# Query and key projections by seven block products, behind the value projections

## The reference, cut to what matters

```
h = rms_norm(x, pre_norm_gain)
proj = h @ w_in                        # (256, 1024) @ (1024, 9344 columns in all)
q, k, v = proj[..., :4608]             # three groups of 8 heads of 64 each: 1536 columns q, 1536 k, 1536 v
#   dilated attention in three groups (stride 1, 4, 16), logits = q k^T / 8 + bias,
#   joined over the groups by one softmax; o_attn * silu(z_attn) @ w_up_attn
r, k, v, w_low, a_low = shifted(proj[..., OFF_RWKV:OFF_RWKV_GATE])
#   RWKV-7 recurrence over the tokens, group norm, bonus; o_rwkv * silu(z_rwkv) @ w_up_rwkv
merged = sigmoid(g_attn) * y_attn + sigmoid(g_rwkv) * y_rwkv
x = x + rms_norm(merged @ w_out, post_norm_gain)
# second block: a projection, a Hyena mixer (filters, transforms, gates), differential attention,
# w_out_2, router, and 16 experts of 1024 x 2816 (gate, up, down), 32 tokens each: some 550 MB of weights
```

## Time and profile before

| | |
|---|---|
| median of 3 runs | 1835.41 us (1835.23 to 1835.87) |
| profiled execution | 1837.94 us, its span 1835.8 us |
| mean granted clock of TensorE | 0.855 of full |
| PE busy | 1375.2 us, 75% |
| PE weight loads busy | 769.3 us, 42% |
| DVE busy | 435.8 us, 24% |
| ACT busy | 144.8 us, 8% |
| POOL busy | 36.4 us, 2% |
| chain that ended last | PE 53%, DMA 33% |
| L890 (project) | 976 instructions of 256 columns, 221.6 us |

### The profile page before, as it was taken

One profiled execution on the slowest core, in us unless ns is written; L12 is line 12 of the kernel. 1 busy time (PEld: TensorE's weight loads), 2 busy tenths in 40 slices (PEclk: granted clock), 3 DMA queues, 4 the chain that ended last, 5 costly groups with the idle time before them and its releaser, 6 DMA issues.

```text
span 1835.8 us, 21606 instructions
## 1 busy us (share of the span) xinstructions
PE 1375.2 (75%) x10034; PEld 769.3 (42%) x10034; DVE 435.8 (24%) x671; ACT 144.8 (8%) x316; POOL 36.4 (2%) x53
## 2 busy tenths in 40 slices
PE   9999999999999865756666674756656575766655
PEld 7888577858665321313222231322322131322311
DVE  3543224357653211010102101010210101021012
ACT  3200012113131000000000000000000000000001
POOL 1001010000000000000000000000000000000000
PEclk9999999999999978777787787878787787778788
DMA  7324363333389999999999999999999999999995
GB/s 256 138 94 144 110 224 117 112 127 111 124 328 392 430 435 429 432 432 428 436 430 431 432 431 430 427 434 432 427 434 432 430 433 426 430 434 431 431 428 238
DMA packets 54909, 629.55 MB, mean 343 GB/s; under 512 B 3546, under 2 KB 4741, under 8 KB 37412
## 3 DMA queue, kind: packets, MB, share of 16 engines
q1 hardware_dynamic: 51952, 620.02, 80.4%
q0 software_dynamic: 2448, 7.82, 1.5%
q10 hardware_dynamic: 420, 0.34, 0.1%
HBM read 627.05 MB, written 1.11 MB: 342 GB/s over the span
## 4 chain that ended last, share of the span: by engine, by line
PE 53%; DMA 33%; another core or an unknown queue 8%; DVE 4%; ACT 1%; issue 1%; POOL 0%; POOLq 0%; DVEq 0%; SPq 0%; ACTq 0%
DMA arena<-in_w_up 25%; PE psum L1453 12%; PE psum L890 12%; PE psum L1503 6%; DMA arena<-in_w_gate 5%; PE psum L1442 4%; PE psum L1232 3%; DMA arena<-in_w_down 3%; PE psum L1162 2%; PE psum L1321 2%; PE psum L893 2%; PE psum L969 1%; DVE arena L2109 1%; PE psum L896 1%; PE psum L1136 1%
## 5 line engine op out<-in xcount | busy, mean ns | idle before, releaser
L1453 PE MATMUL psum<-arena 128*32 128x352 f32 x4096 | 418.8, 573 | 335.3 <-DMA arena<-in_w_up 207.3
L1453 PEld LDWEIGHTS psum<-arena 128*32 128x32 f32 x4096 | 149.7, 133 | 604.4 <-issue 246.2
L1503 PE MATMUL psum<-arena 128*32 128x512 f32 x1408 | 230.7, 729 | 48.0 <-DMA arena<-in_w_down 48.0
L890 PE MATMUL psum<-arena 128*128 128x256 f32 x976 | 221.6, 383 | 1.3 <-ACT arena L601 0.7
L890 PEld LDWEIGHTS psum<-arena 128*128 128x128 f32 x976 | 181.9, 189 | 29.8 <-issue 2.2
L2102 DVE TENSOR_SCALAR arena<-arena 128x704 f32<-128x704 f32 x16 | 8.4, 528 | 639.6 <-ACT arena L836 639.5
L1503 PEld LDWEIGHTS psum<-arena 128*32 128x32 f32 x1408 | 67.1, 128 | 198.2 <-issue 122.9
L2109 DVE TENSOR_TENSOR arena<-psum,arena 128x704 f32<-128x704 f32 x16 | 21.5, 1345 | 318.2 <-PE psum L1453 318.2
L1442 PEld LDWEIGHTS psum<-arena 128*128 128x128 f32 x512 | 93.1, 285 | 1.5 <-issue 1.1
L1442 PE MATMUL psum<-arena 128*128 128x32 f32 x512 | 93.4, 357 | 0.2 <-DVE arena L2066 0.2
L839 ACT ACTIVATE arena<-psum 128x1024 f32<-128x1024 f32 x15 | 15.4, 1024 | 775.1 <-PE psum L1503 775.1
(11 more groups left out here) (373 smaller groups left out, 970.0 us busy)
## 6 DMA issues: line engine op xcount, KB each, us to landing
arena<-in_w_gate SPq DMA_DIRECT2D x22, 5632.0 KB, 53.8
arena<-in_w_up SPq DMA_DIRECT2D x21, 5632.0 KB, 52.1
arena<-in_w_down SPq DMA_DIRECT2D x19, 5632.0 KB, 54.6
arena<-in_w_up SPq DMA_DIRECT2D x21, 2816.0 KB, 48.1
arena<-in_w_down SPq DMA_DIRECT2D x20, 2816.0 KB, 54.1
arena<-in_w_gate SPq DMA_DIRECT2D x20, 2816.0 KB, 50.2
arena<-in_w_in SPq DMA_DIRECT2D x24, 2048.0 KB, 8.7
arena<-in_w_down SPq DMA_DIRECT2D x11, 1408.0 KB, 50.4
```

Source lines behind the costliest of these rows:

```text
L890: last = mm(o, block_of(blk)[:, k, c * P:c * P + P], rhs[:, k, :], start=(k == 0), stop=(k == KC - 1))
L1453: last = mm(psum[32 * j:32 * j + CAP, b + n, 0:HALFQ], XC[:, k, :], region(o, HALFQ), start=(k == 0), stop=(k == KC - 1))
L1503: last = mm(psum[32 * g:32 * g + CAP, gate + 1 - n, :], HT[:, i, :], region(spot(pos), 512), start=(i < 4), stop=(i >= FPP - 4))
```

## The change

For the six blocks q0 to q2 and k0 to k2 the product (512 columns by 1024 features) x (1024 features by 256 tokens) is cut into 2 x 2 blocks (256 columns, 512 features, 128 tokens) and done with seven block products and sums, one level of Strassen's scheme in Winograd's form, in place of eight. Tiles 19 to 42 are now q and k, each block in four parts: A, B and C hold two block products in one bank, D one. GpSimd makes the sums of the weights (S1, S2, and two in place) and of the tokens (T1 to T4, once for hT, once for hR). ScalarE copies the first product of A, VectorE adds all the others out of PSUM. S1, S2 and T1 to T4 take the place of slot 1, so q and k blocks alternate between slots 2 and 0. The value blocks come before q and k, as tiles 13 to 18. The gates, tiles 43 to 50, come behind the chain and all before the transposes of Y. The factor 0.125 moves into `biased`. GpSimd's bias DMAs stand behind its sums.

In the diff below `summed` is one tensor_tensor on GpSimd and a wait for its own end. After the lists and counts come GpSimd's part, ScalarE's (`evac` returns at once for B, C and D), TensorE's and VectorE's. In the state phase whole tiles 37 to 42 stand where halves of 37 to 40 stood, and `halves_added` stands once behind each step of VectorE.

```
+        S1, S2 = region(4096, 4, 256), region(5120, 4, 256)
+        T1, T2, T3, T4 = (region(6144 + 512 * i, 4, P) for i in range(4))
...
+        blocks += [(f"v{i}", in_cols(w_in, 3072 + 512 * i)) for i in range(3)]
         blocks += [(f"q{i}", in_cols(w_in, 512 * i)) for i in range(3)]
         blocks += [(f"k{i}", in_cols(w_in, 1536 + 512 * i)) for i in range(3)]
-        blocks += [(f"v{i}", in_cols(w_in, 3072 + 512 * i)) for i in range(3)]
...
+        SLOTS = (0, 2, 1, 0, 2, 1, 0, 2, 0, 2, 0, 2, 0)
+        def slot_of(n):
+            return SLOTS[n] if n < len(SLOTS) else (n + 1) % NB
+        def tenant_before(n):
+            if blocks[n][0] == "g0":
+                return "k2"
+            return next((blocks[i][0] for i in reversed(range(n)) if slot_of(i) == slot_of(n)), None)
...
+        tiles += [(f"q{i}", c, hT, qT[:, 4 * i:4 * i + 4, :], 1.0) for i in range(3) for c in "ABCD"]
+        tiles += [(f"k{i}", c, hR, kT[:, 4 * i:4 * i + 4, :], 1.0) for i in range(3) for c in "ABCD"]
+        assert (V_TILE, Q_TILE, Z_TILE, G_TILE, NT) == (13, 19, 43, 51, 67)
+        def seven(j):
+            return Q_TILE <= j < Z_TILE
+        def evacs(j):
+            return sum(not seven(i) or tiles[i][1] == "A" for i in range(j + 1))
+        def halves(j):
+            return sum(seven(i) for i in range(j + 1))
+        def sums_at(j):
+            blk, c = tiles[j][0:2]
+            n = SEVEN.index(blk)
+            if blk == "k0":
+                return 23 if c == "B" else 24
+            return 4 + 4 * n + (4 if n > 3 else 0) + (2 if c == "B" else 4)
...
+            def token_sums(h):
+                summed(T1, h[:, 0:4, P:T], h[:, 0:4, 0:P], ALU.subtract)
+                summed(T2, h[:, 4:KC, P:T], T1, ALU.subtract)
+                summed(T3, h[:, 4:KC, P:T], h[:, 0:4, P:T], ALU.subtract)
+                summed(T4, T2, h[:, 4:KC, 0:P], ALU.subtract)
+            def weight_sums(name):
+                w, j = block_of(name), first_of(name)
+                weights_in(pool, name)
+                if j > Q_TILE:
+                    pool.wait_ge(S["proj_ready"], j - 2)
+                summed(S1, w[:, 0:4, T:2 * T], w[:, 4:KC, T:2 * T], ALU.add)
+                summed(S2, S1, w[:, 0:4, 0:T], ALU.subtract)
+                summed(w[:, 0:4, T:2 * T], w[:, 0:4, 0:T], w[:, 0:4, T:2 * T], ALU.subtract)
+                if name == "k0":
+                    pool.wait_ge(S["proj_ready"], j)
+                    token_sums(hR)
+                pool.wait_ge(S["proj_ready"], j + 1)
+                summed(w[:, 4:KC, 0:T], w[:, 4:KC, 0:T], S2, ALU.subtract)
+            pool.wait_ge(S["proj_ready"], first_of("q0"))
+            token_sums(hT)
+            for name in SEVEN:
+                weight_sums(name)
             pool.wait_ge(S["T1_mm"], 5)
...
+                if seven(j):
+                    act.activation(quarter(j, 0, 1), part(j, 0), ACT.Copy).then_inc(S["proj_evac"], 1)
+                    return
...
             from_state(1)
-            evac(36)
-            evac(37)
             from_state(2)
-            evac(38)
+            evac(39)
             from_state(3)
-            evac(39)
-            evac(40)
-            evac(41)
             act.wait_ge(S["mean_in"], 3)
             act.activation(small[:, 64:80], small[:, 64:80], ACT.Sqrt).then_inc(S["root_in"], 1)
-            for j in range(42, 47):
+            for j in range(Z_TILE, 47):
                 evac(j)
...
+            def block_product(j, slot, w, h):
+                for f in range(2):
+                    o = psum[:, bank_of(j), slot * T + f * P:slot * T + f * P + P]
+                    for k in range(4):
+                        last = mm(o, w[:, k, f * P:f * P + P], h[:, k, :], start=(k == 0), stop=(k == 3))
+                return last
+            def seven_products(j):
+                blk, c, h = tiles[j][0:3]
+                w = block_of(blk)
+                if c in "BC":
+                    pe.wait_ge(S["w_sums"], sums_at(j))
+                if c == "A":
+                    block_product(j, 0, w[:, 0:4, 0:T], h[:, 0:4, 0:P])
+                    last = block_product(j, 1, w[:, 4:KC, 0:T], h[:, 4:KC, 0:P])
+                elif c == "B":
+                    block_product(j, 0, S2, T2)
+                    last = block_product(j, 1, S1, T1)
+                elif c == "C":
+                    block_product(j, 0, w[:, 0:4, T:2 * T], T3)
+                    last = block_product(j, 1, w[:, 4:KC, 0:T], h[:, 4:KC, P:T])
+                else:
+                    last = block_product(j, 0, w[:, 4:KC, T:2 * T], T4)
+                last.then_inc(S["proj_ready"], 1)
...
             project(18)
-            project(19)
...
                 if cp:
+                    project(19)
                     project(20)
                     pe.wait_ge(S["gram_done"], 5)
...
             solve(3)
-            project(40, 0, 4)
+            project(43, 0, 4)
             step(3)
-            project(40, 4, 8)
-            for j in range(41, 47):
+            project(43, 4, 8)
+            for j in range(44, G_TILE):
                 project(j)
             pe.wait_ge(S["gn_done"], 1)
...
-            for j in range(47, G_TILE):
-                project(j)
...
+            def halves_added(j):
+                c = tiles[j][1]
+                left, right = part(j, 0), part(j, 1)
+                c11, c12, c21, c22 = (quarter(j, i, t) for i in range(2) for t in range(2))
+                if c == "A":
+                    dve.wait_ge(S["proj_evac"], evacs(j))
+                    last = V.tensor_tensor(c11, right, c12, ALU.add)
+                else:
+                    dve.wait_ge(S["proj_ready"], j + 1)
+                    dve.wait_ge(S["half_read"], halves(j - 1))
+                if c == "B":
+                    link(V.tensor_tensor(c12, left, c12, ALU.add))
+                    last = V.tensor_tensor(c22, right, c12, ALU.add)
+                elif c == "C":
+                    link(V.tensor_tensor(c21, left, c12, ALU.add))
+                    link(V.tensor_tensor(c12, right, c22, ALU.add))
+                    last = V.tensor_tensor(c22, left, c22, ALU.add)
+                elif c == "D":
+                    last = V.tensor_tensor(c21, c21, left, ALU.subtract)
+                last.then_inc(S["half_read"], 1)
...
+                if cp:
+                    halves_added(19)
+                    halves_added(20)
                 dve.wait_ge(S["gram_mm"], 2 * cp + 1)
...
                     link(V.tensor_tensor(flat(mOff), flat(mA), over(OFFB[lev + 1]), ALU.mult))
+                halves_added(24 + 2 * lev)
                 dve.wait_ge(S["MM_mm"], lev + 1)
...
                     mirrored(2 * lev + 4)
+                halves_added(25 + 2 * lev)
...
-                link(V.tensor_tensor(LG[:, i, :, :], psum[:, 2 * i:2 * i + 2, 0:384], bias[:, tile, 2 * p:2 * p + 2, :], ALU.add))
+                link(V.scalar_tensor_tensor(LG[:, i, :, :], psum[:, 2 * i:2 * i + 2, 0:384], 0.125, bias[:, tile, 2 * p:2 * p + 2, :], ALU.mult, ALU.add))
```

More of the change, by code:

```diff
@@ L397, in program, with weights_in @@
         number = {name: n for n, (name, _) in enumerate(blocks)}
+        SLOTS = (0, 2, 1, 0, 2, 1, 0, 2, 0, 2, 0, 2, 0)
+        assert number["v1"] == 5 and number["k2"] == 12
+        def slot_of(n):
+            return SLOTS[n] if n < len(SLOTS) else (n + 1) % NB
         def block_of(name):
-            return wb[(number[name] + 1) % NB]
-        def weights_in(pe, name):
+            return wb[slot_of(number[name])]
+        def weights_in(eng, name):
             n = number[name]
-            pe.wait_ge(wload[(n + 1) % NB], 16 * (n // NB + 1))
+            eng.wait_ge(wload[slot_of(n)], 16 * sum(slot_of(i) == slot_of(n) for i in range(n + 1)))
+        def tenant_before(n):
+            if blocks[n][0] == "g0":
+                return "k2"
+            return next((blocks[i][0] for i in reversed(range(n)) if slot_of(i) == slot_of(n)), None)
         experts = [A[n].rearrange("e (p i) n -> (e p) (i n)", p=P) for n in ("w_gate", "w_up", "w_down")]
@@ L416, in program @@
         tiles += [(f"rkv{i}", c, hT, prT[:, 4 * i + c, :], 1.0) for i in (1, 0, 2) for c in range(4)]
-        Q_TILE = len(tiles)
-        tiles += [(f"q{i}", c, hT, qT[:, 4 * i + c, :], 0.125) for i in range(3) for c in range(4)]
-        tiles += [(f"k{i}", c, hR, kT[:, 4 * i + c, :], 1.0) for i in range(3) for c in range(4)]
         V_TILE = len(tiles)
@@ L439, in program, with first_of @@
         tiles2 += [(f"at{i}", c) for c in range(4) for i in (0, 1)]
+        SEVEN = ("q0", "q1", "q2", "k0", "k1", "k2")
+        def first_of(name):
+            return min(j for j, t in enumerate(tiles) if t[0] == name)
+        def sums_at(j):
+            blk, c = tiles[j][0:2]
+            n = SEVEN.index(blk)
+            if blk == "k0":
+                return 23 if c == "B" else 24
+            return 4 + 4 * n + (4 if n > 3 else 0) + (2 if c == "B" else 4)
         def bank2_of(j):
```

(31 more changed lines are left out.)

61 lines of the change are left out of this document (41 added, 20 removed).

## The result

The changed kernel takes 1841.14 us (median of 7 runs, 1840.52 to 1841.69) against 1835.23 for the kernel before (7 runs in the same comparison, 1834.74 to 1835.87): a ratio of 1.0032 (95% interval 1.0020 to 1.0043), 5.9 us slower. The prediction said 1837.3 with a range of 1830 to 1843. The time lies in the range, but past the 0.2% that were to count as no change, on the side that had a chance of 0.32. All comparisons use fast runs; two executions of the kernel before beside the last four experiments, at 2100.59 and 2702.36 us, are left out.

What follows compares the result with a forecast made beforehand. TensorE was taken to bound the kernel up to about 555 us, the expert stream after it. -8.1 - 0.1 + 3.9 + 3.4 + 0.2 + 2.6 = +1.9 us on 1835.4 gave 1837.3, range 1830 to 1843.

Steps and rivals of the forecast that it cites:

- Parts 1 and 2: TensorE's q and k products and the value tiles moved ahead: -8.1 and -0.1 us for the products, 0 for the moves.
- Part 3: TensorE waits before product B of q0 for six GpSimd sums of 10.2 us: +3.9 us, bounds 0 and 9.8.
- Part 5: Gates behind the chain: TensorE waits at tile 45 for ScalarE's group norm square root and table load, +3.4 us.
- transposes at tile 52: Transposes of Y right before logits(0), VectorE doing orT and zaT before the first biased: +0.2 us.
- Part 4: VectorE's adds, seven a block at 0.42 us, and ScalarE's evacuations are covered by TensorE's work: 0.
- Part 6: TensorE's clock falls behind each of the two new waits, three in four, 1.7 us a fall: +2.6 us.
- rival (b): TensorE's clock stays down longer, 6.8 us behind each wait, losing 3.4 each: 1841.5 us; chance 0.14.
- Part 1: Seven products a block, 112 instructions at 0.1115 us for 64 at 0.2162: -8.1 us over six blocks, another -0.1 for placing.
- Rival (d): Products don't save what they say: at 0.124 us an instruction of 128 columns no gain, 1845.4 us; chance 0.03.
- (a): GpSimd is fast: its six sums end before B, only the second wait is left, 1830.8 to 1832.5 us; chance 0.18.
- (c): GpSimd is slow, 3.75 ns an element: waits of 9.8 + 1.6 in place of 3.9, 1844.8 us; chance 0.09.
- Rival (e): One of the two waits is hidden by something not seen: 1832.6 or 1832.1 us; chance 0.14.

Runs made afterwards that it cites:

- the last four experiments: Changed kernel, waits filled with matmuls: 1836.9 us; its order with eight products: 1835.3; kernel before with 16 GpSimd adds: 1836.04; with 16 copies: 1836.5.
- the four kernels that have them: The changed kernel, and it with one edit: tile 18 earlier, 1836.01 us; tiles 43 and 44 evacuated earlier, 1836.09; q1's sums held back, 1837.08.
- the kernel with eight products: The changed kernel's tile order with the plain product, no sums or adds, tiles 43 and 44 evacuated before the square root: 1835.3 us.
- the three together: The changed kernel with tile 18 before the bonus matmuls, tiles 43 and 44 evacuated before the square root, q1's sums held back: 1827.84 us.

## Why the prediction was right or wrong

| step | predicted | measured |
|---|---|---|
| Parts 1 and 2, products and moves | -8.2 | -7.5 (products -7.9, moves +0.4) |
| Part 3, first wait | +3.9 | +3.8 |
| Part 5, second wait | +3.4 | +3.15 |
| Part 5, transposes at tile 52 | +0.2 | 0 |
| Part 4, VectorE's additions | 0 | +2.2 |
| Part 6, clock | +2.6 | +4.2 (4.7 by the medians) |
| sum | +1.9 | +5.9 |

That the time lies in the range is partly luck: the range reached that far up for rival (b), a clock that stays down longer, while the miss of 3.8 us is as large as a wait that no rival had, with its fall of the clock (2.2 + 1.6).

**Part 4 failed**, at the words "If such cover were gone, each place would cost what the adds last, 0.4 to 1.4 us. I put 0." It took VectorE's durations from the trace of before, where GpSimd is nearly idle in this stretch, and added up VectorE's own load. The adds did fit, if only just: all of them are in the experiment that holds back q1's sums, and they cost TensorE 0.2 us there, not 2.2. The part names the places where the cover is tightest; tile 23, behind tile 21's three additions, is not among them, and there it was used up. What did not stay was the duration of a VectorE instruction beside a busy GpSimd. The critical one grew from 1.22 to 3.27 us. The state phase itself had no such wait, as predicted; the third wait stands just ahead of the levels, a place for which the prediction had no sign of its own. The Trainium skill, SBUF — State Buffer, section "SBUF: two separate sides", states the rule that the prediction should have weighed: a VectorE instruction with two SBUF inputs and a GpSimd instruction that reads SBUF share a pair of ports under an exclusive lock, and whoever starts second waits until the first is through. The trace agrees: 2.05 us of delay that end with GpSimd's sum, none where an input is in PSUM, and a GpSimd mean of 2.57 us in place of 2.36 where the two are mixed.

**Part 6 was mis-sized**, 2.6 for 4.2. More than a third of it (1.6) is Part 4's again, since the third wait has its own fall of the clock. The price of a wait, 0.75 x 1.7 = 1.3 us, is near what the runs show (1.4 to 1.6), and three waits by it give 3.9. The trace has the fall behind six of the nine idle waits of 2.2 to 3.8 us in the four kernels that have them, the price being 1.6 to 2.6 us when it comes. Which wait it follows is not fixed: the one at tile 45 has none in the changed kernel and one in two experiments. The Trainium skill, TensorE: Matmul & The Clock Gate, part 1, has idling take the clock back, and the prediction read that as a fall behind each wait. These traces don't bear that reading out at this length of wait: three of the nine have none. What settles it for a single wait stays open.

**Part 1.** 2 x 4 matmuls a product and 7 products a block are as counted. An instruction is 0.1117 us from the next, (3.84 - 0.377) / 31, where 0.1115 was taken, and D, 16 instructions, takes 2.05, with 1.98 to the start of what follows (238.31, 240.29). Six blocks of 112 instructions at 0.1117 in place of 64 at 0.2162 make 8.0. The bill has 7.5, and the 0.4 us between them is what the changed order costs by itself in the trace of the kernel with eight products (553.87 against 553.49). Rival (d) is out.

**Part 3** was right in structure and in size: six sums took 9.8 us (108.19 to 118.02; 10.2 predicted), 1024 elements 2.36 (2.33), 512 elements 1.28 and 1.10 by turns (1.36). The chain of waits lays them end to end ahead of the product:

```profile
112.07 1.10 POOL arena L587
...
113.24 2.36 POOL arena L587
115.67 2.35 POOL arena L587
...
118.15 6.40 PE psum L966 x32
```

Its estimate from a one-input and a strided copy was good; rivals (a) and (c) are out. The later blocks' sums are covered as it said, their bias DMAs too (issued from 228.55).

**Part 5** was right: step(3) ends at 246.29, the table load and the first evacuation stand where it put them, and TensorE restarts 8.6 us behind (233.3 - 224.67 = 8.6 predicted). ScalarE's timeline:

```profile
252.57 0.22 ACT L756 ACTIVATE arena<-arena 128x16 f32<-128x16 f32 x1 [13.54 <-DVE arena L1826]
252.81 1.28 ACT L705 ACT_TABLE_LOAD   x1
254.10 0.39 ACT L705 ACTIVATE arena<-psum 128x256 f32<-128x256 f32 x1
```

The 0.2 us at tile 52 did not come: the wait ahead of it is 0.56 us where it was 0.57, and the distance to the kernel before is 5.9 us in front of it and behind it. Rival (e), one of the two waits hidden, is out: both are in the trace, and the second went when ScalarE's order was changed. Rival (b) is the nearest in its number (1841.5), and for half of its reason: the clock did stay down 6.8 us behind the first wait in the profiled execution. It was down 3.4 behind the others, or not at all, so as a rule it did not hold; the number came from a third wait.

**The end of the span.** That a microsecond of TensorE's before 555 us is one of the end is borne out: +5.9 at 559.39 and +5.9 on the medians; for the three together, against the changed kernel, -12.9 in the trace (546.45) and -13.3 on the medians. The spans of the two profiled executions, 3.0 apart, show it less well.

## What to carry to other kernels

Work that is moved to an idle GpSimd is not free for VectorE: look for VectorE instructions with both inputs in SBUF on the critical chain, and start GpSimd's instructions behind them or well before. Such a delay costs nothing where VectorE has cover, and its full length where added work has used the cover up. A sum that TensorE needs wants a full latency of head start (here 10 us for six), so find out first what it may start on. In a stretch where TensorE has no idle time, a new wait of 2 to 4 us costs its length plus, here, some 1.5 us of clock on average.

## What the runs showed of the hardware

- VectorE with two SBUF inputs and GpSimd reading SBUF take turns by whole instructions: 1.22 us became 2.07 to 3.27, and another of 256 elements 1.10 where 0.42 to 0.43 is usual. An input in PSUM, or a transpose of one input, is untouched (1.23 and 1.25 us beside GpSimd's adds).
- GpSimd's fp32 sum of two SBUF inputs: 2.36 us for 1024 elements a partition, 1.10 or 1.28 for 512; a copy of 1024, 1.15.
- The granted clock falls behind some idle times of 2.2 to 3.8 us in an otherwise dense stretch and not behind others (six of nine). Where it fell it was at 1.2 GHz for 3.4 us in five cases and 6.8 in one; filling the three waits with matmuls that nobody needs made the kernel 4.2 us faster, although one of the waits became half a microsecond longer.
